# Expert stage in quads of experts with column groups of 32, and a ring of 1 MB halves

## The chip, the cores and the metric

The kernel runs on one core of one Trainium2 chip. The metric is the device time of one execution, in microseconds.

## What is computed

The reference is one inference step of a two-layer decoder trunk for 256 prompt tokens and 8 decode tokens, model width 1024, all in f32. Layer 0 mixes tokens with GLA and Mamba-2, layer 1 with HGRN2. After each mixer comes a mixture of experts: 16 experts in four routing groups of four, each token goes to two experts of its best group. Only this part is touched by the change:

```python
for e in range(N_EXPERTS):                       # 16
    he = jax.nn.silu(t @ w_gate[e]) * (t @ w_up[e])   # 1024 -> 512
    y = y + gates[:, e:e + 1] * (he @ w_down[e])      # 512 -> 1024
x = layer_norm(ALPHA * x + y, ...)
```

The weights of one expert are three matrices of 2 MB (2.10 million bytes), those of a layer 96 MB in 48 matrices, or 96 halves of 1 MB (1,048,576 bytes).

## The kernel before

Each engine runs its own program and they meet at semaphores. SyncE (SP) issues all weight loads in program order (`fill`, L337; `fill_half`, L346): a load first waits until its place is free, and whatever stands behind it on SP waits too. The places are the six 2 MB slots of `ring` (`PLACE`) and, in the expert stages alone, a seventh, `EXTRA`, in the buffer `A`.

An expert stage (`experts`, PE) runs like this. After layer norm the router's scores are turned into places: five small matmuls count, for each token, its row among the tokens of its expert (`moe_places`), `keep_clock(4)` issues eight filler instructions (L1180), DVE builds one-hot matrices `SLOT1` (L2303). `gather` (L1205, four per layer, each for four experts) multiplies them with the tokens; the result is `xg`, 64 rows for each expert: 56 for prompt tokens, 8 for the decode tokens. The 16 experts are worked in eight pairs; the two experts of a pair lie in the two column groups of 64 of the array. A pair is `gate_up` (L1220, 64 instructions: a f32 matmul is two instructions), `turn_hidden` (L1229, four transposes), `down` (L1244, 32 instructions), with the `scatter` of the previous pair (L1259, 16 instructions) in two halves around `turn_hidden`. `scatter` multiplies the pair's 128 result rows with `PT`, the transposed gate weights, over all 264 tokens, in eight chunks; DVE adds each chunk to `xacc` (L2410, eight instructions of 264 columns a pair). In every second pair the `gather` for the next four experts stands ahead of `down`. `turn_weights` builds `PT` in the first pair.

After the last pair DVE takes the row means of the result (`centred_copy`), DVE and ACT copy it without its mean to `Y`, the last `scatter` runs, ACT squares `xacc` chunk by chunk and PE sums the squares (L1143), and the layer norm follows. Weights of the next stage (`w_c`) are issued by SP behind those of the experts; all but the first of them wait for the layer norm (`norm_roots`).

## Time and profile before

| | us |
|---|---|
| median of 3 runs (lowest to highest) | 989.76 (989.46 to 990.78) |
| span of the profiled execution | 988.7 |
| PE busy in it | 952.2 (96%) |
| DVE / ACT / POOL busy | 400.9 / 281.5 / 103.6 |
| DMA moved | 299.64 MB, mean 303 GB/s |
| chain that ended last: PE / DMA / DVE | 78% / 10% / 7% |

The span is the time from the first to the last instruction; the median of the runs is 1.1 us longer. Matmuls overlap one another, so that the busy time of a group of instructions is less than count times mean. Of a group's cost on PE the chain's pieces tell more: they are laid end to end. The first expert stage lies at about 304 to 544 us of the span, the second at 741 to 981 us.

### The profile page before, as it was taken

What the parts mean: (1) busy time and instruction counts of PE and PEld (TensorE: products, weight loads), DVE (VectorE), ACT (ScalarE), POOL (GpSimd) and SP (SyncE); (2) the same over time, 40 slices, a digit from 0 to 9 for tenths busy, and PEclk for the clock granted to TensorE, in tenths of its full rate; (3) what the DMA queues carried; (4) which work ended last, traced back from release to release, by engine and by line L of the source; (5) the groups of instructions that cost most, each with busy time, mean ns of one, the idle gap of its engine ahead of it and who ended that gap; (6) DMA issues with size and microseconds to landing.
All of it is one profiled execution on the core that took longest, in us unless ns stands there. A gap on an engine that the chain in (4) does not pass through costs nothing.

```text
span 988.7 us, 12651 instructions
## 1 busy us (share of the span) xinstructions
PE 952.2 (96%) x4923; PEld 609.8 (62%) x4923; DVE 400.9 (41%) x973; ACT 281.5 (28%) x603; POOL 103.6 (10%) x167
## 2 busy tenths in 40 slices
PE   8999999899999999999998999999999999999995
PEld 6777777677876354545435877777875444545433
DVE  2468886954127021212116336675244111212134
ACT  3534434223024110101002258886133010101003
POOL 2222223361000000000000000113100000000000
PEclk9999999999999999999999999999999999999998
DMA  9943545966843999999993954342885999999981
GB/s 380 357 193 134 191 161 171 407 266 266 340 164 147 423 410 422 421 423 420 421 422 153 409 221 174 152 149 71 329 352 237 421 413 421 420 422 420 422 351 45
DMA packets 38991, 299.64 MB, mean 303 GB/s; under 512 B 4808, under 2 KB 6344, under 8 KB 8456
## 3 DMA queue, kind: packets, MB, share of 16 engines
q1 hardware_dynamic: 33696, 268.52, 66.7%
q0 software_dynamic: 4544, 29.65, 7.8%
q8 instruction: 43, 0.70, 0.3%
q10 hardware_dynamic: 688, 0.60, 0.2%
q14 instruction: 20, 0.16, 0.0%
HBM read 283.32 MB, written 15.53 MB: 302 GB/s over the span
## 4 chain that ended last, share of the span: by engine, by line
PE 78%; DMA 10%; DVE 7%; ACT 3%; issue 2%; POOL 0%; ACTq 0%; DVEq 0%; POOLq 0%
PE bank L1220 20%; PE bank L1244 10%; PE bank L1390 7%; PE bank L856 7%; PE bank L1103 6%; PE bank L1259 6%; PE bank L1205 5%; PE bank L1377 4%; DMA ring<-in_w_up 4%; PE bank L1124 3%; PE bank L1143 2%; DVE ring L2093 1%; DMA W<-in_conv_cols 1%; DMA spread<-xd_rows 1%; DMA spread<-v_rows 1%
## 5 line engine op out<-in xcount | busy, mean ns | idle before, releaser
L1220 PE MATMUL bank<-ring,A 128*64 128x512 f32 x880 | 223.0, 592 | 1.0 <-DMA ring<-in_w_up 1.0
L856 PE MATMUL bank<-xT,ring 128*128 128x264 f32 x704 | 165.0, 390 | 1.7 <-DMA ring<-in_w_ab 1.3
L856 PEld LDWEIGHTS bank<-xT,ring 128*128 128x128 f32 x704 | 132.0, 191 | 32.3 <-issue 8.9
L1220 PEld LDWEIGHTS bank<-ring,A 128*64 128x64 f32 x880 | 72.5, 137 | 123.8 <-issue 123.1
L1244 PE MATMUL bank<-ring,W 128*64 128x512 f32 x448 | 113.8, 596 | 0.9 <-ACT W L1741 0.9
L2364 DVE TENSOR_TENSOR W<-W,bank 128x512 f32<-128x512 f32 x16 | 11.0, 688 | 200.3 <-PE bank L1220 200.3
L1390 PE MATMUL bank<-xT,ring 128*128 128x264 f32 x320 | 78.0, 391 | 0.0
L1244 PEld LDWEIGHTS bank<-ring,W 128*64 128x64 f32 x448 | 34.8, 137 | 60.4 <-issue 59.3
L1259 PE MATMUL bank<-W,A 128*128 128x264 f32 x256 | 66.9, 408 | 3.9 <-ACT A L1733 3.9
L1390 PEld LDWEIGHTS bank<-xT,ring 128*128 128x128 f32 x320 | 58.3, 190 | 11.1 <-issue 1.6
L1220 PE MATMUL bank<-A 128*64 128x512 f32 x144 | 63.4, 592 | 0.7 <-DMA ring<-in_w_up 0.7
L1259 PEld LDWEIGHTS bank<-W,A 128*128 128x128 f32 x256 | 48.5, 199 | 24.5 <-issue 11.4
L2410 DVE TENSOR_TENSOR W<-W,bank 128x264 f32<-128x264 f32 x128 | 54.3, 428 | 12.5 <-PE bank L1259 11.3
L1103 PE MATMUL bank<-A,ring 128*128 128x264 f32 x256 | 57.4, 386 | 0.3 <-ACT A L1472 0.3
L781 POOL TENSOR_SCALAR xT<-xT,vecs 128x264 f32<-128x264 f32 x4 | 5.6, 1398 | 492.7 <-DVE xT L2214 492.7
L1103 PEld LDWEIGHTS bank<-A,ring 128*128 128x128 f32 x256 | 48.6, 190 | 8.8 <-ACT A L1472 0.6
L1720 ACT ACTIVATE W<-bank 128x512 f32<-128x512 f32 x16 | 9.6, 597 | 145.2 <-PE bank L1220 145.2
L1205 PE MATMUL bank<-A,W 128*128 128x224 f32 x256 | 49.9, 353 | 0.6 <-DVEq L2312 0.6
L2374 DVE COPY A<-bank 128x512 f32<-128x512 f32 x14 | 9.7, 692 | 99.0 <-PE bank L1244 99.0
L1205 PEld LDWEIGHTS bank<-A,W 128*128 128x128 f32 x256 | 48.3, 190 | 1.4 <-DVEq L2312 1.0
L1377 PE MATMUL bank<-xT,ring 128*128 128x264 f32 x192 | 44.6, 396 | 2.6 <-ACT xT L1663 2.6
L1724 ACT COPY W<-bank 128x512 f32<-128x512 f32 x16 | 9.4, 585 | 124.0 <-PE bank L1229 124.0
(339 smaller groups left out, 1147.2 us busy)
## 6 DMA issues: line engine op xcount, KB each, us to landing
ring<-in_w_gate SPq DMA_DIRECT2D x56, 1024.0 KB, 13.8
ring<-in_w_down SPq DMA_DIRECT2D x56, 1024.0 KB, 14.0
ring<-in_w_up SPq DMA_DIRECT2D x54, 1024.0 KB, 16.8
ring<-in_w_ab SPq DMA_DIRECT2D x10, 2048.0 KB, 8.4
ring<-in_w_c SPq DMA_DIRECT2D x8, 2048.0 KB, 11.2
A<-in_w_up SPq DMA_DIRECT2D x10, 1024.0 KB, 14.3
ring<-in_w_oab SPq DMA_DIRECT2D x4, 2048.0 KB, 10.4
A<-in_w_gate SPq DMA_DIRECT2D x8, 1024.0 KB, 13.2
```

The source lines that it names most:

```text
L856: mm = pe.matmul(ab_bank(m)[:, 0:T], slot(AB_IN0 + m // 4, 8)[:, c, (m % 4) * P:(m % 4 + 1) * P], xT[:, c, :], start=(c == 0), stop=(c == ...
L1103: mm = pe.matmul(out_bank(m)[:, 0:T], w[:, c, (m % 2) * P:(m % 2 + 1) * P], src, start=(c == 0), stop=(c == 15))
L1124: mm = pe.matmul(out_bank(m)[:, 0:T], w[:, c, (m % 4) * P:(m % 4 + 1) * P], A[:, 16 + c, :], start=(c == 0), stop=(c == 7))
L1143: mm = pe.matmul(square_bank(k)[:, 0:T], ones[:, :], lnsq[:, c, :], start=(c == 0), stop=(c == DC - 1))
L1205: mm = pe.matmul(gather_bank(i)[:, c * 4 * PCAP:(c + 1) * 4 * PCAP], xtm[:, b, (2 * i + c) * P:(2 * i + c + 1) * P], SLOT1[:, b, 4 * g:4 * ...
L1220: mm = pe.matmul(bank[i][64 * j:64 * j + 64, :], xg[:, 2 * (pair % 2) + j, c, :], slot(n0 + 6 * pair + 2 * i + j, 8)[:, c, :], start=(c == ...
L1244: mm = pe.matmul(bank[4 + i][64 * j:64 * j + 64, :], hT[:, f * P + CAP * j:f * P + CAP * (j + 1)], slot(n0 + 6 * pair + 4 + j, 8)[:, 4 * i ...
L1259: pe.matmul(back_bank(c)[:, 0:T], Y[:, c * P:(c + 1) * P], PT[:, pair, :], start=True, stop=True).then_inc(sem("moe_back"), 1)
L1377: mm = pe.matmul(c_bank(m)[:, 0:T], slot(n, 8)[:, c, i * P:(i + 1) * P], xT[:, c, :], start=(c == 0), stop=(c == DC - 1))
L1390: mm = pe.matmul(c_bank(m)[:, 0:T], slot(c_in(m // 4), 8)[:, c, (m % 4) * P:(m % 4 + 1) * P], xT[:, c, :], start=(c == 0), stop=(c == DC - 1))
L2364: dve.tensor_tensor(hid, hid, bank[1][:, :], ALU.mult).then_inc(sem("moe_hidden"), 1)
L2410: dve.tensor_tensor(xacc[:, c, :], xacc[:, c, :], back_bank(c)[:, 0:T], ALU.add).then_inc(sem("moe_added"), 1)
```

## The change

The 16 experts are worked in four quads. A quad holds one expert of each routing group, and each has one of four column groups of 32. The prompt tokens are taken in two blocks of 128, and each block goes through the array by itself: an expert has 32 rows for a block, 28 for prompt tokens and 4 for half of the decode tokens (before: 56 and 8 for all). If an expert gets more prompt tokens of a block than 28, an overflow path runs, as it did before above 56; no expert gets more than 25 of a block with these inputs. The places come from two matmuls in place of five. A gather has 112 columns moving in place of 224, a scatter matmul 136 in place of 264 (one block and the decode tokens); there are as many of each. Up to three scatter chunks share a bank, and DVE adds them with two instructions, one for the block's tokens and one for the decode tokens.

On PE a quad is now `gate_up(q, 0)`, `gate_up(q, 1)`, `turn_hidden` of block 0, `gather(q + 1)`, `turn_hidden` of block 1, `down` in two halves, `scatter(q)`. The mean that the layer norm needs ahead of the last scatter moves in front of the last quad's up projection.

The weight ring has 1 MB halves as its unit. Twenty places ("homes") take the first twenty halves of a layer: twelve in `ring`, five in `A`, one each in `spread`, in the place of `xacc` and in that of `Y`; the last two are used once, so the ring then goes round over 18. Half k waits for the read of the group of four halves in which half k-18 lies. The first loads wait for the ends of the users of those buffers in the mixer (`home_free`).

```diff
-CAP = 64
-PCAP = CAP - NB
-PLIM = PCAP
-DR = 64
+QUADS = E_N // E_G
+ROWS = P // E_G
+DCAP = NB // 2
+PCAP = ROWS - DCAP
+SPREAD_N = P + NB
+SCATTER = ((0, 3), (3, 6), (6, 8))
...
-        EXTRA = Aflat[:, 7232:7232 + SLOT_W]
...
+        MOE_HALVES = 6 * E_N
+        QUAD_HALVES = MOE_HALVES // QUADS
+        A_HOMES, SPREAD_HOME, XACC_HOME, Y_HOME = range(12, 17), 17, 18, 19
+        FIRST_HOMES = [
+            [XACC_HOME, Y_HOME, SPREAD_HOME, 12, 14, 15, 8, 9, 10, 11, 4, 5, 6, 7, 2, 3, 0, 1, 13, 16],
+            [XACC_HOME, Y_HOME, 4, 5, 6, 7, SPREAD_HOME, 12, 13, 15, 16, 2, 3, 0, 1, 8, 9, 10, 11, 14]]
+        FIRST_ORDER = [list(range(20)), [2, 3, 4, 5, 0, 1] + list(range(6, 20))]
+        CYCLE = len(FIRST_HOMES[0]) - 2
+        HOMES = [[h[k] if k < 2 else h[2 + (k - 2) % CYCLE] for k in range(MOE_HALVES)] for h in FIRST_HOMES]
+        FILLS = 6
...
+        def halves_read(layer, q, i, half):
+
+            return 6 * (QUADS * layer + q) + 2 * i + half + 1
...
+        def down_bank(i, b):
+
+            return bank[4 + b] if i else up_bank(b)
+
+        def back_bank(n):
+
+            return bank[2 + n % 2]
...
+            def home_free(layer, home):
+
+                if home < 2 * SLOTS:
+                    slot_free = ({4: ("states_stored", 64), 5: ("states_stored", 64), 2: ("out0_ready", 2), 3: ("out0_ready", 4),
+                                  1: ("out0_ready", 6), 0: ("out0_ready", 8)},
+                                 {2: ("in1_ready", 28), 3: ("in1_ready", 32), 1: ("states_stored", 96), 0: ("states_stored", 96),
+                                  4: ("out1_ready", 4), 5: ("out1_ready", 8)})
+                    return [slot_free[layer][home // 2]]
+                if layer == 0:
+                    if home in (13, 16):
+                        return [("out0_ready", 8)]
+                    return [("ssd_outputs_read", 4), ("heads_gated", 4), ("ssd_p_stored", 32)]
+                if home == 14:
+                    return [("out1_ready", 8)]
+                return [("heads_gated", 12), ("heads_prompt_state_stored0", 16 * 6), ("heads_prompt_state_stored1", 16 * 6)]
+
+            def fill_expert(layer, k):
+
+                q, r = divmod(k, QUAD_HALVES)
+                i, r = divmod(r, 8)
+                half, g = divmod(r, 4)
+                home = HOMES[layer][k]
+                if k < len(FIRST_HOMES[layer]):
+                    for name, value in home_free(layer, home):
+                        sp.wait_ge(sem(name), value)
+                else:
+                    sp.wait_ge(sem("moe_read"), MOE_HALVES // 4 * layer + (k - CYCLE) // 4 + 1)
+                src = expert_views(layer, bass.ds(E_G * g + q, 1))[i]
+                n = halves_read(layer, q, i, half) - 1
+                sp.dma_start(home_of(home), src[:, HALF_W * half:HALF_W * (half + 1)]).then_inc(
+                    sem(f"moe_filled{n % FILLS}"), 16)
...
+        xg = area(2112, DC, 2 * E_G, ROWS)
+        xacc = area(4160, DC, T)
+        Y = area(6272, 2, D)
+        PT = area(8320, 2 * QUADS, SPREAD_N)
...
-                pe.matmul(bank[3][:, 0:16], strict[:, :], chosen[:, 0, :], start=True, stop=True)
-                for i, last in enumerate((strict[:, :], ones[:, :])):
-                    pe.matmul(bank[3][:, 16 + 16 * i:32 + 16 * i], ones[:, :], chosen[:, 0, :], start=True, stop=False)
-                    mm = pe.matmul(bank[3][:, 16 + 16 * i:32 + 16 * i], last, chosen[:, 1, :], start=False, stop=True)
-                mm.then_inc(sem("moe_places"), 1)
+                pe.matmul(bank[3][:, 0:2 * E_N], strict[:, :], chosen[:, 0:2, :], start=True, stop=True)
+                pe.matmul(bank[3][:, 2 * E_N:4 * E_N], ones[:, :], chosen[:, 0:2, :], start=True, stop=True).then_inc(
+                    sem("moe_places"), 1)
                 keep_clock(4)
-                def gather(g):
+                L0 = QUADS * layer
...
                         for c in range(2):
                             for b in range(2):
-                                mm = pe.matmul(gather_bank(i)[:, c * 4 * PCAP:(c + 1) * 4 * PCAP],
+                                at = (2 * c + b) * E_G * PCAP
+                                mm = pe.matmul(gather_bank(i)[:, at:at + E_G * PCAP],
                                                xtm[:, b, (2 * i + c) * P:(2 * i + c + 1) * P],
-                                               SLOT1[:, b, 4 * g:4 * g + 4, 0:PCAP], start=(b == 0), stop=(b == 1))
+                                               SEL[:, q, b, :, 0:PCAP], start=True, stop=True)
                         mm.then_inc(sem("gather_ready"), 1)
...
+                def gate_up(q, i):
+
+                    for half in range(2):
+                        expert_ready(pe, layer, q, i, half)
+                        w = [expert_half(layer, q, i, half, g) for g in range(E_G)]
+                        for b in range(2):
+                            out = up_bank(b) if i else gate_bank(b)
+                            for c in range(4 * half, 4 * half + 4):
+                                if i == 0 and b == 0 and c % 2 == 0:
+                                    pe.wait_ge(sem(f"xg_copied{c // 2 % 2}"), 2 * (L0 + q) + c // 4 + 1)
+                                for g in range(E_G):
+                                    mm = pe.matmul(out[ROWS * g:ROWS * (g + 1), :], xg[:, c, E_G * b + g, :], w[g][:, c % 4, :],
+                                                   start=(c == 0), stop=(c == DC - 1))
+                            if b == 0 and half == 1:
+                                mm.then_inc(sem("block_done"), 1)
+                        mm.then_inc(sem("moe_read"), 1)
...
+                def down(q, i):
+
+                    expert_ready(pe, layer, q, 2, i)
+                    w = [expert_half(layer, q, 2, i, g) for g in range(E_G)]
+                    for b in range(2):
+                        if i == 0:
+                            pe.wait_ge(sem("hT_copied"), 2 * (L0 + q) + b + 1)
+                        elif q + 1 < QUADS:
+                            pe.wait_ge(sem(f"xg_copied{b}"), 2 * (L0 + q + 1) + 1)
                         for f in range(4):
-                            for j in range(2):
-                                mm = pe.matmul(bank[4 + i][64 * j:64 * j + 64, :], hT[:, f * P + CAP * j:f * P + CAP * (j + 1)],
-                                               slot(n0 + 6 * pair + 4 + j, 8)[:, 4 * i + f, :],
+                            for g in range(E_G):
+                                mm = pe.matmul(down_bank(i, b)[ROWS * g:ROWS * (g + 1), :],
+                                               hT[:, b, f * P + ROWS * g:f * P + ROWS * (g + 1)], w[g][:, f, :],
                                                start=(f == 0), stop=(f == 3))
-                        mm.then_inc(sem("moe_down"), 1)
-                        if pair == PAIRS - 1 and i == 0:
-                            pe.wait_ge(sem("norm_ahead"), 3 * layer + 2)
-                            pe.matmul(mean_bank(2 * layer + 1)[:, 0:T], mean_ones[:, :], late_sums[:, 0, :],
-                                      start=True, stop=True).then_inc(sem("norm_sum"), 1)
-
...
+                        mm.then_inc(sem("moe_read" if b else "block_done"), 1)
...
+                def scatter(q):
+
+                    for b in range(2):
+                        for j, (c0, c1) in enumerate(SCATTER):
+                            n = 6 * q + 3 * b + j
+                            if j < 2:
+                                y_ready(q, b, j)
+                            if b == 0 and j < 2 and q + 1 < QUADS:
+                                pe.wait_ge(sem(f"xg_copied{j}"), 2 * (L0 + q + 2))
+                            if n >= 2:
+                                pe.wait_ge(sem("moe_added"), 48 * layer + 2 * (n - 1))
+                            for c in range(c0, c1):
+                                mm = pe.matmul(back_bank(n)[:, (c - c0) * SPREAD_N:(c - c0 + 1) * SPREAD_N],
+                                               Y[:, b, c * P:(c + 1) * P], PT[:, 2 * q + b, :], start=True, stop=True)
+                            mm.then_inc(sem("moe_back"), 1)
...
+                for q in range(QUADS):
+                    gate_up(q, 0)
+                    if q == 0:
+                        turn_weights()
+                        flag = pe.value_load(over[0:1, 0:1], min_val=0, max_val=1)
+                    if q + 1 == QUADS:
+                        pe.wait_ge(sem("norm_ahead"), 4 * layer + 2)
+                        pe.matmul(mean_bank(2 * layer + 1)[:, 0:T], mean_ones[:, :], late_sums[:, 0, :],
+                                  start=True, stop=True).then_inc(sem("norm_sum"), 1)
+                    gate_up(q, 1)
+                    turn_hidden(q, 0)
+                    if q + 1 < QUADS:
+                        gather(q + 1)
+                    turn_hidden(q, 1)
+                    down(q, 0)
+                    down(q, 1)
+                    scatter(q)
...
+                def centred_copies():
+
+                    q = QUADS - 1
+                    for i in range(2):
+                        dve.wait_ge(sem("block_done"), 4 * (L0 + q) + i + 3)
+                        st.add(dve.tensor_reduce(row_means[:, 0, i:i + 1], down_bank(i, 0)[:, :], AX, ALU.add))
+                        if i:
+                            block_mean(0)
+                        dve.wait_ge(sem("moe_read"), halves_read(layer, q, 2, i))
+                        st.add(dve.tensor_reduce(row_means[:, 1, i:i + 1], down_bank(i, 1)[:, :], AX, ALU.add))
+                    block_mean(1)
+                    dve.tensor_scalar(Y[:, 1, 0:512], down_bank(0, 1)[:, :], row_means[:, 1, 2:3], None, ALU.add).then_inc(
+                        sem("y_copied1"), 1)
...
+                def add_back(q):
+                    for b in range(2):
+                        for j, (c0, c1) in enumerate(SCATTER):
+                            n = 6 * (L0 + q) + 3 * b + j
+                            dve.wait_ge(sem("moe_back"), n + 1)
+                            if n >= 3:
+                                dve.wait_ge(sem("moe_added"), 2 * (n - 2))
+                            back = back_bank(n)[:, 0:(c1 - c0) * SPREAD_N].rearrange("p (c t) -> p c t", t=SPREAD_N)
+                            for part, of in ((slice(P * b, P * (b + 1)), slice(0, P)), (slice(NP, T), slice(P, SPREAD_N))):
+                                dve.tensor_tensor(xacc[:, c0:c1, part], xacc[:, c0:c1, part], back[:, :, of], ALU.add).then_inc(
+                                    sem("moe_added"), 1)
```

## Rows read from the trace of the kernel before

**Rows 1.** The profile page, part 2: the span in 40 equal slices of 24.7 us, in tenths.
```profile
DMA  9943545966843999999993954342885999999981
```

**Rows 2.** The chain that ended last, by pieces in order of time: start us, us, what.
```profile
423.36 13.73 PE bank L1220 x64
...
462.04 1.98 PE bank L1259 x8
...
466.24 6.05 PE bank L1205 x32
472.29 7.02 PE bank L1244 x32
479.31 13.76 PE bank L1220 x64
...
747.22 13.88 PE bank L1220 x64
```

**Rows 3.** Timeline of PE around both expert stages: start us, us, line; idle before in brackets.
```profile
297.96 2.40 PE L1180 MATMUL bank<-causal,ident 128*128 128x128 f32 x20
304.03 6.32 PE L1205 MATMUL bank<-A,W 128*128 128x224 f32 x32 [0.31 <-DVEq L2312]
310.28 13.95 PE L1220 MATMUL bank<-ring,A 128*64 128x512 f32 x64
515.56 3.65 PE L1220 MATMUL bank<-ring,A 128*64 128x512 f32 x16 [1.00 <-DMA ring<-in_w_up]
527.57 3.65 PE L1244 MATMUL bank<-ring,W 128*64 128x512 f32 x16
533.18 5.51 PE L1259 MATMUL bank<-W,A 128*128 128x264 f32 x16 [1.96 <-ACT A L1733]
538.53 3.72 PE L1143 MATMUL bank<-A,ones 128*128 128x264 f32 x16
964.16 3.65 PE L1244 MATMUL bank<-ring,W 128*64 128x512 f32 x16
976.32 3.83 PE L1143 MATMUL bank<-A,ones 128*128 128x264 f32 x16 [1.03 <-ACT A L1674]
```

**Rows 4.** Windows around the experts: length, busy time and count of each engine, PEclk, DMA share, GB/s.
```profile
300.00:310.00 10.00, 8.60 (x53) 8.22 (x52) 8.72 (x28) 3.87 (x9) 1.44 (x1) 1.00 0.01 4
450.00:500.00 50.00, 50.00 (x240) 24.36 (x237) 10.57 (x23) 4.88 (x9) 0.00 (x0) 1.00 1.01 421
700.00:750.00 50.00, 47.56 (x261) 39.14 (x261) 25.73 (x72) 15.88 (x28) 3.84 (x8) 1.00 0.77 313
```

**Rows 5.** Timeline of SP's DMA issues ahead of the two expert stages.
```profile
247.10 2.06 SPq L346 DMA_DIRECT2D ring<-in_w_gate  x4
...
289.07 0.70 SPq L346 DMA_DIRECT2D A<-in_w_gate  x1
313.98 0.33 SPq L346 DMA_DIRECT2D ring<-in_w_gate  x1
700.59 0.33 SPq L346 DMA_DIRECT2D A<-in_w_up  x1
```

**Rows 6.** The source view of L346, its last line, for a load of 1 MB.
```profile
DMA to landing us min/median/max: 5.0/14.6/25.7
```

**Rows 7.** PE around line 1079, four column groups of 32 with 512 columns moving.
```profile
186.23 1.92 PE L1079 MATMUL bank<-ring,W 128*32 128x512 f32 x16 [1.81 <-DVE ring L2093]
188.09 2.05 PE L856 MATMUL bank<-xT,ring 128*128 128x264 f32 x8
```

**Rows 8.** One-us windows of PE after the first expert stage: length, busy, PEclk, DMA share, GB/s.
```profile
534.00:535.00 1.00, 1.00 (x4) 0.58 0.00 0
537.00:538.00 1.00, 1.00 (x5) 0.71 0.00 0
```

**Rows 9.** Groups of instructions kept apart by shape: busy us, mean ns, idle before.
```profile
L2387 DVE TENSOR_TENSOR W<-W,bank 128x2112 f32<-128x2112 f32 x2 | 4.7, 2354 | 0.0
L2410 DVE TENSOR_TENSOR W<-W,bank 128x264 f32<-128x264 f32 x128 | 54.3, 428 | 12.5 <-PE bank L1259 11.3
```

More of the change, by code:

```diff
@@ L358, in fill_over, with fill_experts @@
+            def fill_experts(layer):
+                for k in FIRST_ORDER[layer]:
+                    fill_expert(layer, k)
+                for k in range(len(FIRST_ORDER[layer]), MOE_HALVES):
+                    fill_expert(layer, k)
             def fill_over(layer):
@@ L377, in _ @@
                 sp.dma_start(xT[:, c:c + 4, :], x_cols[:, c:c + 4, :]).then_inc(sem(f"x_loaded{c // 4}"), 16)
-            for half in range(2):
-                fill_half(AB_IN0, half, w_ab[0])
+            fill_first(w_ab[0])
             for g in range(11):
@@ new lines, in turn_weights @@
+                def turn_weights():
+                    pe.wait_ge(sem("moe_weighted"), layer + 1)
+                    for r in range(2 * QUADS):
+                        out = bank[(4, 5, 2)[r // 3]][:, (r % 3) * SPREAD_N:(r % 3 + 1) * SPREAD_N]
+                        pe.transpose(out[:, 0:P], WS[:, r * P:(r + 1) * P], ident[:, :])
+                        tr = pe.transpose(out[:, P:SPREAD_N], WS2[:, r * P:(r + 1) * P], ident[0:NB, 0:NB])
+                    tr.then_inc(sem("pt_turned"), 1)
@@ L2382, in sum_ahead @@
                     dve.sem_inc(sem("norm_ahead"), 1)
+                    dve.wait_ge(sem("norm_sum"), 4 * layer + 3)
+                    st.run(minus_mean())
                 def minus_mean():
@@ new lines, in experts @@
+                flag = dve.value_load(over[0:1, 0:1], min_val=0, max_val=1)
+                for q in range(QUADS):
+                    hidden(q)
+                    if q + 1 < QUADS:
+                        for i in (1, 3):
+                            gathered(dve, affine, i, L0 + q + 1)
+                        copies(q)
+                    else:
+                        centred_copies()
+                    add_back(q)
+                    if q + 2 == QUADS:
+                        sum_ahead()
@@ L2422, in experts @@
+                dve.wait_ge(sem("moe_added"), 12 * (L0 + QUADS))
                 with dve.If(flag > 0):
```

467 lines of the change are left out of this document (195 added, 272 removed).

## Prediction

> **What bounds the kernel now.** I read four views in this order. The slices of the page first [rows 1]: the DMA engines are full (9) in two long stretches, slices 13 to 20 and 31 to 37, which are the two expert stages, and mostly idle in the slices just ahead of each. The windows say the same in numbers: 0.01 of the DMA engines at 300 to 310 us and 0.77 at 700 to 750, and 421 GB/s at full share inside [rows 4]. Then the chain, for what PE does meanwhile [rows 2]: inside the stage it is PE, pieces laid end to end. Two pairs last 479.31 - 423.36 = 55.95 us: twice 13.73 (gate and up), 7.02 (down) and 4.20 (scatter and turning, 466.24 - 462.04), and once 6.05 (gather). Last the timeline, for what PE waits for [rows 3]: in all of the stage it stood still on a load just once, for 1.00 us, on the last up matrix.
>
> So the two run level. At 421 GB/s a half of 1,048,576 bytes takes 2.49 us (2.5 below), a pair's twelve halves 29.9 us, while PE needs 28.0 us on average. PE gains some 2 us on the loads with each pair, and the seven slots (14 halves) loaded ahead are used up just in the last pair. From the first gate matmul (310.28) to the end of the last down (527.57 + 3.65 = 531.22) it is 220.9 us. Whoever makes only PE faster meets the loads. What can shorten the stage is more weights loaded in the idle DMA time ahead of it; a faster PE is needed beside it.
>
> **The change: what PE does in a quad.** Gate and up are 256 instructions in fours. The nearest row is the same shape, four groups of 32 with 512 columns: 16 instructions from 186.23 to the next at 188.09, less the first load (0.1, an estimate) 0.43 to 0.46 us a four [rows 7]; I take 0.43, by which the old pair's 32 twos also go (13.73 / 32); at 0.46 PE would end the stage, at 211, 3 us a layer later. So 64 x 0.43 = 27.5 us, the same as two pairs now. Down is 32 fours, taken at twice the old 7.02 = 14.0 us. Turning is eight transposes, 0.12 each as below, 0.9. A gather has half the columns, but a full 128 x 128 load for each instruction; with 128 columns moving, twenty take 2.40 us, 0.12 each [rows 3], so 32 x 0.12 = 3.8 us in place of 6.05. The ends are 3.0 (by columns alone) and 6.05 (the old row, [rows 2]); the twenty are nearest in shape. Scatter is 32 instructions, again 3.8 us, in place of two pairs' 2 x 4.20 less the turning, 7.5. DVE's share of it: its cost goes as 0.155 us + 1.04 ns a column (428 ns for 264, 2354 for 2112 [rows 9]). Three chunks of 128 are 0.55 us and of 8 are 0.18, two chunks 0.42 and 0.17, so two blocks cost 2 x (2 x 0.73 + 0.59) = 4.1 us, in two alternating banks behind its last copy: I take 4.5 us for the scatter. Sum: 27.5 + 14.0 + 0.9 + 3.8 + 4.5 = 50.7 us in place of 55.95. Turning the gate weights is 16 transposes, 2 us, in quad 0.
>
> **The start.** Three count matmuls fewer are six instructions of 0.12, 0.7 us, and one one-hot instruction fewer on DVE hides behind the filler matmuls. The first gather is 2.5 us shorter. The first gate matmul thus comes some 3.4 us earlier, at 306.8 in place of 310.28. ACT and DVE copy the gathered tokens two chunks at a time beside it, and the first weights have long landed.
>
> **The loads, layer 0.** Before, 14 halves are in place, the last of them issued at 289.07 and the next only at 313.98, when the first read ends [rows 5]. Now twenty. The new first waits (`ssd_p_stored` and its like) hold SP, with all twenty halves and the overflow check queued behind, until the mixer's last stores. Before, SP began at 247.10 [rows 5], when its states were stored; sixteen halves (40 us) fit between that and 289, when the last out-projection read opens the last four homes. Their loads take 10 us, so all twenty are in by about 300, before 306.8. Six halves more, 15 us of DMA, lie in idle time.
>
> From here I count from the first gate matmul. Groups of four halves are read at 7.0 and 13.9 us. Halves 20 and 21 may start at 7.0, the next only at 13.9; a lone half lands 5.0 us after its issue, of which 2.5 is transfer [rows 6]. So group 5 (halves 20 to 23) is complete at 13.9 + 2.5 + 5.0 = 21.4, and each further group 10.0 us later: group 23, the last down halves, at 201.4. PE by itself would start that group at 3 x 50.7 + 2 + 27.5 + 0.9 + 0.7 + 7.0 = 190.3. (The 0.7 is the wait for block 1's hidden rows, which in the last quad no gather covers.) So loads end the stage: PE waits about 3 us before several groups of the last quad, and the last down ends at 201.4 + 7.0 = 208.4, or 515.2 us of the span. PE has 11 us in hand, so its prices may be wrong by 5% without moving the end.
>
> **Those waits and the clock.** After 1.96 us of idle PE at 531 to 533 the granted clock is at half, 1.2 of 2.4 GHz, from about 534.2 to 537.6 [rows 8], and sixteen instructions take 5.51 us [rows 3] in place of the 3.7 of a scatter (4.20 less four transposes, [rows 2]); after the wait of 1.00 us nothing is lost, 3.65 us for sixteen [rows 3]. So waits of 3 us will halve the clock for a while. In the middle this costs nothing, as PE then waits less for the next group; before the last group it costs about 1.75 us (3.4 us at half). I take half: 0.9. The stage ends at 516.1 in place of 531.2: 15.1 us saved.
>
> **Layer 1.** Before, four halves are out by 700.59 [rows 5]; the other sixteen need 40 us of DMA, and other transfers 12 more (313 GB/s for 50 us [rows 4] is 15.7 MB, of which ten halves are 10.5; 5.2 MB at 421 are 12 us). From 700 the DMA engines are thus busy until 752. The first gate matmul moves from 747.2 [rows 2] to 743.8, so group 1 is read at 757.7, halves 20 and 21 land by 757, and group 5 is complete at 765.2, the last at 945.2, the last down 0.9 late at 953.1. Before it was 964.16 + 3.65 = 967.8 [rows 3]. 14.7 us saved. This uses the times of before for what lies ahead and adds to layer 0's gain, which carries through: the mixer between is a chain of PE, and the first `w_c` load waits for nothing new.
>
> **The tail.** Before, from the end of the last down to the end of the squares' sum it is 542.25 - 531.22 = 11.0 us, and 980.15 - 967.8 = 12.3 in layer 1 [rows 3]: a wait of 1.96, a scatter of 5.5 and 3.7 of sums among it. Now block 0's rows are ready while down runs on block 1, and scatter starts without a wait. DVE comes free some 2.0 us after down (two reductions' work and a copy), adds six pieces in 4.1 us, PE's last chunks end at about 5.8, the sums (32 instructions of 0.12) at 9.6. Saved 1.5 and, with the second copy's wait gone, 2 us; if the clock falls here too, nothing.
>
> **Sum.** 15.1 + 14.7 + 1.5 + 2.0 = 33.3 us of the span of 988.7, so 955.4, and with the 1.1 us by which the runs' median lies above the span, 956.5 us.
>
> The rivals.
> - **A refill that stumbles.** SP's waits, at most two groups ahead, may leave the DMA engines short gaps that the old, finer order did not. Half of the six halves' gain lost would be 2 x 7.5: 971. Against it: 4 groups lie between a home's read and its next use, 40 us of loads. 0.15.
> - **No more ahead than before.** If the first homes open late (layer 0's wait for stores) SP holds all twenty behind them. Then 15 us a layer go: 986. The order suits the dates known, so 0.07.
> - **PE sets the end after all.** If the loads run ahead (a gap less at the start, up to 427 GB/s), the end is PE's, 8 to 11 us a layer earlier at most: 938. No row shows more than 421 over 50 us. 0.06.
> - **Clock at half through the last quad (slower).** Every group then lasts 14.0 us against 10.0 of loads. From group 20, which comes at 171.4: 185.4, 199.4, 215.9, 229.9 us; 21 us a layer more than 208.4, so 998. It decides from 17 us a layer. Against it: the clock came back within 4 us of steady work [rows 8]. 0.05. The Trainium skill, "TensorE: Matmul & The Clock Gate", section HAM oscillation, tells of a kernel in which each short burst of matmuls after a DMA wait started with a gated clock, every time. By that rule this rival would be the likeliest; the trace's own bursts here are 7 us, not 2, and agree with it only for the start of a burst.
> - **Fours that do not overlap (slower).** If over a long run each four shows one weight load, 0.12 us more as in the twenty, 0.55 a four, then a quad is 96 x 0.55 + 9.2 = 62 us, longer than its loads, the last down ends at 2 + 4 x 62 - 4.5 = 245.5, and that is 37 us a layer above 208.4: 1030. It decides from 0.50 us a four. The row has only sixteen in sequence. 0.05. The Trainium skill, "TensorEngine Tiling (Array Packing)", section PSUM Bottleneck, warns that evacuation may become the bound after such packing; here DVE has 4.1 us of adds, four instructions of 512 columns (0.69) and four of 224 (0.39) in a quad of 50 us, and ACT as many without the adds, so I give it no price.
>
> **How the numbers follow.** The forecast has 0.60, its own range 948 to 965 (both clock losses, 0.46 a four, the start). The rivals above have 0.15, 0.07, 0.06, 0.05 and 0.05, 0.02 is left for no change. A measurement here can tell 0.2% (2 us) from no change: faster 0.88, same 0.02, slower 0.10. The range of 8 in 10 takes the forecast, the stumbling refill and most of the PE case: 942 to 973.
>
> **What would show it.** Right: PE idle, with DMA as its releaser, about 1 to 3 us before four or five groups in the last quad of each layer; DMA at 421 GB/s without a gap from 21 us after the first gate matmul to the end of the loads; a quad of about 51 us on PE until then; the last loads about 15 us earlier. Wrong: more than 0.45 us a four, DMA gaps inside the stage, fewer than twenty halves in at the first gate matmul, or PE never waiting for DMA.

## The result and the profile after

The changed kernel takes 966.22 us (median of 4 runs, 963.58 to 969.02), beside 989.61 us for the kernel before on the same chip: ratio 0.976, interval 0.974 to 0.979, so 23.4 us less. The forecast was 956.5 us, in a range of 942 to 973. The profiled execution took 964.11 us, with a span of 962.3. One execution of the kernel before, beside the first four experiments, took 1662.55 us at a granted clock of 0.556, and no median or ratio below counts it.

The slices of the profile page of the changed kernel, for [rows 1]; a slice is 24.1 us here:

```profile
DMA  9953453985983999999993954343799999999951
```

The two long stretches of full DMA engines are still there. Ahead of them the idle time is used: slice 12 has gone from 4 to 8 (layer 0's loads ahead), slice 31 from 5 to 9 (layer 1's).

The chain that ended last, of the changed kernel, for [rows 2] (start us, us, what). Its lines are: L1266 gather, L1282 gate and up, L1306 down, L1332 scatter, L1205 the sums of squares.

```profile
301.43 3.83 PE bank L1266 x32
305.25 13.87 PE bank L1282 x128
...
359.57 27.61 PE bank L1282 x256
...
391.76 13.87 PE bank L1306 x128
410.44 27.65 PE bank L1282 x256
440.69 28.37 DMA ring<-in_w_gate
469.10 7.12 PE bank L1282 x64
481.84 26.93 DMA A<-in_w_down
508.82 7.12 PE bank L1306 x64
...
727.10 13.87 PE bank L1282 x128
...
900.48 29.98 DMA ring<-in_w_down
930.50 8.81 PE bank L1306 x64
947.84 5.44 PE bank L1205 x32
```

A quad lasts 410.44 - 359.57 = 50.87 us on PE, where a pair of pairs lasted 55.95. In the last quad the chain goes over to DMA, at 440.69 and 481.84 and again at 900.48. The last group of loads is there 508.82 - 305.25 = 203.6 us after the first gate matmul, in layer 1 930.50 - 727.10 = 203.4.

The waits of PE in the changed kernel, summed up (total us, times, longest):

```profile
PE bank L1282 <- DMA ring<-in_w_up: 8.5, 4, 2.9
PE bank L1306 <- DMA A<-in_w_down: 4.2, 2, 2.8
...
PE bank L1205 <- issue: 3.0, 1, 3.0
PE bank L1306 <- DMA ring<-in_w_down: 2.8, 1, 2.8
...
PE bank L1282 <- DMA ring<-in_w_gate: 0.8, 1, 0.8
...
PE bank L1282 <- DMA A<-in_w_gate: 0.5, 1, 0.5
```

Where [rows 3] had one wait of 1.00 us for a load, there are now nine in the five groups of DMA, 16.8 us, all in the last quads: five in layer 0 and four in layer 1. The timeline of PE at the two ends, for the end of [rows 3] (start us, us, line; idle before in brackets):

```profile
515.82 1.66 PE L1332 MATMUL bank<-W 128*128 128x136 f32 x12
518.40 3.04 PE L1332 MATMUL bank<-W 128*128 128x136 f32 x20 [0.92 <-DVE W L2498]
521.28 3.80 PE L1205 MATMUL bank<-W,ones 128*128 128x128 f32 x32
...
947.84 5.42 PE L1205 MATMUL bank<-W,ones 128*128 128x128 f32 x32 [3.02 <-issue]
```

And the windows, for [rows 4] and [rows 8] (length, PE busy and its count, PEclk, DMA share, GB/s):

```profile
296.00:298.00 2.00, 2.00 (x20) 1.00 0.80 336
300.00:310.00 10.00, 9.77 (x90) 1.00 0.01 2
...
312.00:314.00 2.00, 2.00 (x24) 1.00 0.39 66
318.00:320.00 2.00, 2.00 (x17) 1.00 0.54 221
330.00:332.00 2.00, 2.00 (x24) 1.00 0.96 320
450.00:500.00 50.00, 44.06 (x374) 0.97 1.01 421
700.00:750.00 50.00, 47.65 (x365) 1.00 0.99 410
480.00:481.00 1.00, 1.00 (x12) 0.50 1.02 426
948.00:950.00 2.00, 2.00 (x10) 0.50 0.04 8
```

The loads made ahead end at 298 us; up to 312 DMA stands still; then the refill starts, with dips at 318 and at 330 us. In layer 1 the share from 700 to 750 us is 0.99 in place of 0.77. So the stage is bound by its loads, as forecast, and it is shorter, since more was loaded in idle time: from the first gate matmul to the end of the last down it was 220.9 and 220.6 us, and is 515.94 - 305.25 = 210.7 and 939.31 - 727.10 = 212.2.

### The profile page after: what moved, and what is told of

It is laid out like the page before. It is cut to its first block, busy times and chain, and to the rows that moved or that the text cites. A ratio compares the mean times of both kernels' runs of the same rounds, so it can differ in the third digit from the quotient of the medians.

```text
span 962.3 us, 15639 instructions
## 1 busy us (share of the span) xinstructions
PE 910.4 (95%) x6463; PEld 561.9 (58%) x6463; DVE 372.9 (39%) x947; ACT 278.4 (29%) x591; POOL 103.7 (11%) x168
## 4 chain that ended last, share of the span: by engine, by line
PE 68%; DMA 17%; DVE 8%; ACT 2%; issue 2%; SPq 1%; POOL 1%; ACTq 0%; DVEq 0%; POOLq 0%
PE bank L1282 19%; PE bank L1459 8%; PE bank L1306 7%; PE bank L911 7%; PE bank L1158 6%; PE bank L1446 5%; DMA A<-in_w_gate 3%; DMA ring<-in_w_down 3%; DMA ring<-in_w_gate 3%; DMA A<-in_w_down 3%; PE bank L1179 3%; PE bank L1332 3%; PE bank L1266 2%; DVE ring L2173 1%; DMA spread<-v_rows 1%
## 5 line engine op out<-in xcount | busy, mean ns | idle before, releaser
L1282 PE MATMUL bank<-ring,W 128*32 128x512 f32 x1312 | 184.8, 603 | 6.8 <-DMA ring<-in_w_up 6.3
L911 PEld LDWEIGHTS bank<-xT,ring 128*128 128x128 f32 x704 | 131.3, 190 | 31.4 <-issue 8.5
L1282 PE MATMUL bank<-A,W 128*32 128x512 f32 x544 | 119.3, 593 | 3.0 <-DMA ring<-in_w_up 2.2
L1282 PEld LDWEIGHTS bank<-ring,W 128*32 128x32 f32 x1312 | 51.1, 111 | 103.5 <-issue 93.0
L1306 PE MATMUL bank<-ring,A 128*32 128x512 f32 x672 | 99.6, 604 | 4.2 <-DMA ring<-in_w_down 2.8
L1306 PE MATMUL bank<-A 128*32 128x512 f32 x304 | 70.2, 593 | 0.0
L1459 PEld LDWEIGHTS bank<-xT,ring 128*128 128x128 f32 x320 | 58.3, 190 | 11.1 <-issue 1.6
L1306 PEld LDWEIGHTS bank<-ring,A 128*32 128x32 f32 x672 | 27.1, 111 | 56.0 <-issue 50.5
L1282 PE MATMUL bank<-spread,W 128*32 128x512 f32 x128 | 56.3, 593 | 0.0
L1282 PEld LDWEIGHTS bank<-A,W 128*32 128x32 f32 x544 | 31.2, 110 | 35.6 <-issue 31.1
L1446 PEld LDWEIGHTS bank<-xT,ring 128*128 128x128 f32 x192 | 37.1, 195 | 9.8 <-issue 2.6
L1332 PE MATMUL bank<-W 128*128 128x136 f32 x256 | 37.9, 292 | 2.7 <-DVE W L2498 1.8
L1332 PEld LDWEIGHTS bank<-W 128*128 128x128 f32 x256 | 31.9, 189 | 13.8 <-issue 8.1
```

Of the source, the lines that this page charges most:

```text
L911: mm = pe.matmul(ab_bank(m)[:, 0:T], slot(AB_IN0 + m // 4, 8)[:, c, (m % 4) * P:(m % 4 + 1) * P], xT[:, c, :], start=(c == 0), stop=(c == ...
L1282: mm = pe.matmul(out[ROWS * g:ROWS * (g + 1), :], xg[:, c, E_G * b + g, :], w[g][:, c % 4, :], start=(c == 0), stop=(c == DC - 1))
L1306: mm = pe.matmul(down_bank(i, b)[ROWS * g:ROWS * (g + 1), :], hT[:, b, f * P + ROWS * g:f * P + ROWS * (g + 1)], w[g][:, f, :], start=(f = ...
L1332: mm = pe.matmul(back_bank(n)[:, (c - c0) * SPREAD_N:(c - c0 + 1) * SPREAD_N], Y[:, b, c * P:(c + 1) * P], PT[:, 2 * q + b, :], start=True ...
L1446: mm = pe.matmul(c_bank(m)[:, 0:T], slot(n, 8)[:, c, i * P:(i + 1) * P], xT[:, c, :], start=(c == 0), stop=(c == DC - 1))
L1459: mm = pe.matmul(c_bank(m)[:, 0:T], slot(c_in(m // 4), 8)[:, c, (m % 4) * P:(m % 4 + 1) * P], xT[:, c, :], start=(c == 0), stop=(c == DC - 1))
```

## The experiments

All are edits of the changed kernel, and each computes the same result; where unused matmuls are added, they go to a bank that nobody reads then, and this is said. A stage is counted from the first gate matmul to the end of the last down (L0 and L1 for the two layers). The first four ran beside the kernel before at 989.14 us, the next four beside 990.05, the last three beside 988.65.

**Fourteen homes in place of twenty.** Only the loads made ahead are taken back; the quads stay.

```diff
-            [XACC_HOME, Y_HOME, SPREAD_HOME, 12, 14, 15, 8, 9, 10, 11, 4, 5, 6, 7, 2, 3, 0, 1, 13, 16],
+            [XACC_HOME, Y_HOME, 8, 9, 10, 11, 4, 5, 6, 7, 2, 3, 0, 1],
...
-        FIRST_ORDER = [list(range(20)), [2, 3, 4, 5, 0, 1] + list(range(6, 20))]
+        FIRST_ORDER = [list(range(14)), [2, 3, 4, 5, 0, 1] + list(range(6, 14))]
```

> The changed kernel with only 14 homes (the ring's twelve halves, xacc and Y), as many halves loaded ahead as before; quads and PE work untouched. Theory (loads end the stage; what the change gained is the six more halves loaded in idle time): the last down halves land 6 x 2.5 = 15 us later in each layer, so about 15 us later end of each expert stage, 30 us in all, near 994 us, a little above the kernel before; PE waits for DMA 20 us or more a layer. Rival (the lighter gather and scatter on PE gave the gain): within 3 us of the changed kernel's 966.

Measured: 995.4 us (median of 8, 993.51 to 999.58), ratio 1.007 (1.004 to 1.009) to the kernel before. Its chain:

```profile
307.42 13.87 PE bank L1282 x128
...
415.47 21.01 DMA ring<-in_w_up
...
444.98 22.77 DMA ring<-in_w_down
...
476.24 21.30 DMA ring<-in_w_up
497.59 7.12 PE bank L1282 x64
506.04 21.27 DMA ring<-in_w_down
527.36 8.81 PE bank L1306 x64
```

From 415 us on nearly every group ends in a DMA, and PE waits 22.2 and 19.1 us for loads. The stage is 228.75 us in L0 and 225.5 in L1, 18.1 and 13.3 longer than with twenty. So without the six halves nothing of the gain is left: the faster quads alone, with their coarser ring, give none.

With fourteen halves loaded ahead, as before, the quads are even 7.8 and 4.9 us slower than the pairs (220.9 and 220.6). The last load lands 219.9 and 218.3 us after the first gate matmul, before 215.1 and 214.7. These 4.8 and 3.6 us are lost for the most part at the first refills, where DMA has dips at 320 to 324 and at 332 us; from then on a group lands about every 9.9 us, a few excepted. Homes come free four halves at a time and not two, and two of the fourteen are used only once (before, all fourteen went round); these two causes aren't told apart. The rest stands behind the last load: 8.8 and 7.2 us of down work, where before it was 5.8 and 5.9; of the 8.8, 1.7 us is the clock.

**PE slowed, with twenty homes and with fourteen.** After the scatter of quads 0 to 2 unused matmuls are put in: 10, or 22 (4.91 us, by which a quad is as long as the old pairs).

```diff
                     scatter(q)
+                    if q + 1 < QUADS:
+                        keep_clock(22)
```

> The changed kernel with 20 filler instructions (0.12 us each, 2.4 us) on PE behind the scatters of quads 0 to 2, 7.2 us more PE work in each layer. Theory (PE has about 6.6 us in hand per layer: 8.3 us of DMA waits less 1.75 of clock): no more than 1 us a layer later, and the waits for DMA in the last quad nearly gone; 964 to 968 us. Rival (PE bounds): 14 us more, 980.

> The changed kernel with 44 filler instructions (5.3 us) behind the scatters of quads 0 to 2, which gives PE the pace that it had before, 56 us for four experts; twenty homes. Theory: 15.8 us more PE work a layer, of which 6.6 are covered: 9 us later in each layer less up to 1.75 of clock, about 980 to 984 us; no waits for DMA on PE. Rival (the lighter PE work gave everything): 988 or more. Rival (prefetch gave everything): 966.

> Both: 14 homes and the fillers of 5.3 us. Theory: with 14 homes PE has 6.6 + 15 = 21.6 us in hand, more than the 15.8 of fillers, so no later than with 14 homes alone, about 991 to 995 us. If the two parts simply added it would be 966 + 30 + 18 = 1010.

Measured: 972.02 us (967.81 to 974.01) with ten, 972.0 (968.74 to 972.75) with 22, and 999.19 (997.49 to 1002.85) with 22 and fourteen homes. With ten, the last group of L0 starts 510.43 - 306.35 = 204.1 us after the first gate matmul, 0.5 later than in the changed kernel, and the stages are 211.2 and 212.3 us: the work is hidden, as expected. The whole was expected at 964 to 968 and missed this, and 8.3 of the 16.8 us of waits for loads are left, where they should have nearly gone. The longer time lies outside the stages: 214.6 us between them in place of 211.2 (a wait of 1.81 us, below, and layer 1's first gather at half clock, 5.45 us in place of 3.83), a start 1.1 us later and a tail 1.5 us longer. With 22 the chain is PE's to the end:

```profile
306.83 13.87 PE bank L1282 x128
...
492.14 13.92 PE bank L1282 x128
507.54 13.92 PE bank L1306 x128
```

The stage is 214.6 us in both layers, 3.9 and 2.4 more for 14.7 us of work put in. I had expected 9: I had taken the clock's loss off the room that PE has, where it must be added, since a PE that never waits never loses it. The room is 14.7 - 3.9 = 10.8 us in L0 and 12.3 in L1. With fourteen homes the same 14.7 us cost 1.9 and 2.0 (stages of 230.6 and 227.5): the effects don't add, and DMA is the bound. I had expected no cost at all there and at most 995 us. In L0 a new dip of DMA stands at 372 to 376 us, and the last down takes 10.00 us in place of 8.81; what of the 1.9 us each makes wasn't tried.

The fillers stand behind three of the four quads, so this is not quite the old pace: the last quad keeps the new one. With 4.9 us more in it the stage would be 219.5 us, an estimate from these rows, and nearly all of its gain gone. Twenty homes with the old pairs were not run.

**The dips at the start of the refill.** The changed kernel's last group lands 2 us later than forecast, and DMA has the dips at 318 to 322 and at 330 us above. Two edits were tried alone, then together. One puts the homes that are used only once (`xacc`, `y`) at halves 4 and 5, so that all four halves of group 0 open homes. The other moves the turning of the gate weights from behind the first expert's up halves to between them, so that the first up half is read without the turning, 3.3 us, ahead of it. (The first also lets ACT write `xacc` a group later; the second reads the overflow flag in quad 1.)

```diff
-        HOMES = [[h[k] if k < 2 else h[2 + (k - 2) % CYCLE] for k in range(MOE_HALVES)] for h in FIRST_HOMES]
+        HOMES = [[home_at(h, k) for k in range(MOE_HALVES)] for h in FIRST_HOMES]
...
                     for half in range(2):
                         expert_ready(pe, layer, q, i, half)
+                        if (q, i, half) == (0, 1, 1):
+                            turn_weights()
...
-                    if q == 0:
-                        turn_weights()
```

> The changed kernel with the two homes that are used once (xacc and Y) taken by halves 4 and 5 in place of 0 and 1, so that the first group read (7 us after the first gate matmul) sets free four homes in place of two; ACT writes xacc one group later. Theory (the end follows from when the loads may start again): the DMA engines lose no 2 us gap at 13 us after the first gate matmul, and the last down ends about 2 us earlier in each layer (208.5 to 209 us after the first gate matmul in place of 210.7 in layer 0). Rival (the gap is made good later, since SP has four groups in hand): no change of the stage's length.

> The changed kernel with the turning of the gate weights (3.3 us of PE) moved from ahead of the first quad's up projection to between its two halves, so that up half 0 is read 3.3 us earlier. PE's work is the same. Theory: halves 26 and later may start 3.3 us earlier, a gap of about 1.5 us in the loads around 24 us after the first gate matmul goes, the stage ends 1 to 1.5 us earlier in each layer. Rival (only PE's total work counts): no change.

> Both edits of the two kernels before it that gained nothing alone: the four halves used once stand in the second group, so the fifth quarter-megabyte pair of homes comes free after the first four reads, and the turn of the routing weights is put between the two up halves of the first expert. Theory (the 2 us that the last group lands late come from the dips of the queue at 312 to 330 us, and each edit alone only moved the dip from the one wait to the other): no dip below 405 GB/s between 318 and 335 us, last group 200 to 202 us after the first gate matmul in place of 203.6, stage 2 to 3 us shorter per layer, whole 960 to 963 us. Rival (the rate after the dip, 410 GB/s, is what sets the landing, or the queue makes the dip good): last group again at 203 to 204 us, whole 964 to 967.

> The changed kernel once more, beside the two others of this call on one chip, so that they are compared with it and not with a run of another chip. Expected: 964 to 968 us; last group of each layer 203.6 us after the first gate matmul; tail of layer 1 (end of the last down to end of the square sums) 13 to 14 us.

Measured, with the time at which the last group starts after the first gate matmul in L0 and L1:

| | median us (range) | last group |
|---|---|---|
| changed kernel, first chip | 966.22 (963.58 to 969.02) | 203.6, 203.4 |
| homes alone | 964.96 (963.51 to 968.92) | 203.7, 203.5 |
| turning alone | 965.62 (964.16 to 969.3) | 203.8, 203.1 |
| changed kernel again | 967.83 (964.58 to 968.63) | 205.3, 204.3 |
| both | 962.83 (960.41 to 964.5) | 202.0, 202.1 |

The chain of the kernel with both edits (its first gate matmul is at 304.95):

```profile
479.81 27.10 DMA A<-in_w_down
506.96 7.12 PE bank L1316 x64
```

Each alone leaves one of the two dips and gains nothing: with the homes alone it lies at 330 us, with the turning alone at 320. The landings of single loads in the trace say the same. Group 5 (halves 20 to 23) and group 6 are complete 21.5 and 33.2 us after the first gate matmul of layer 0 in the changed kernel, 20.9 and 32.9 with the homes alone, 21.9 and 32.7 with the turning alone, and 21.0 and 30.9 with both. Both together leave no dip, and the last group lands some 1.4 us sooner. The whole is 5.0 us faster than the changed kernel on the same chip; only 2 x 1.4 of it is this. The rest differs from run to run: the start of the first stage (304.95 in place of 307.23) and the clock.

**No jump ahead of the last sums.** In layer 0 the sums of squares stand in the branch that PE takes (`flag < 1`); in layer 1 behind the overflow code, over which PE jumps. The edit puts layer 1's in the branch too.

```diff
...
-                if layer == 0:
-                    with pe.If(flag < 1):
-                        norm_squares(1)
+                with pe.If(flag < 1):
+                    norm_squares(2 * layer + 1)
+                    if layer == 0:
                         settle_over()
                 over_experts(layer, flag)
-                if layer == 1:
-                    norm_squares(3)
```

> The changed kernel with the sums of the squares of layer 1 issued in the branch that is taken when nothing overflows, as in layer 0, so that PE doesn't jump over the overflow code between the last scatter and the sums. Theory (PE's idle time of 3.0 us there, which the profile puts to issue, is fetching instructions behind the jump): this idle time goes to about 1 us, the clock isn't lowered behind it, 2 to 4 us less from the last down to the end of the sums in layer 1 (14.0 us in the changed kernel, 9.2 in layer 0). Rival (PE waits there for the squares or for the clock): unchanged.

Measured: 961.66 us (961.08 to 962.25), ratio 0.972 (0.969 to 0.975). Its timeline of PE at the end of layer 1:

```profile
946.41 3.80 PE L1205 MATMUL bank<-W,ones 128*128 128x128 f32 x32
```

The wait of 3.02 us is gone, and so is the slow clock behind it (3.80 us in place of 5.42). From the end of the last down to the end of the sums it is 950.21 - 941.06 = 9.2 us, in the changed kernel 953.26 - 939.31 = 14.0. In the changed kernel one packet of the instruction queue falls into that wait; this is the queue's row of DMA at 944 to 948 us:

```profile
q8 instruction: 1, 0.02, 1.4%
```

Without the jump there is none from 936 to 948 us. The wait is that for the code on the other side of the jump.

**The clock kept through the last quad.** Unused matmuls, 8, 10, 4 and 10 calls of two instructions, ahead of the two up and the two down halves of quad 3, where PE waits for loads.

```diff
...
+                        if (q, i, half) == (3, 1, 1):
+                            keep_clock(10, 3)
...
+                        keep_clock(8, 3)
...
+                    if q + 1 == QUADS:
+                        keep_clock(4, 3)
                     down(q, 0)
+                    if q + 1 == QUADS:
+                        keep_clock(10, 3)
                     down(q, 1)
```

> The changed kernel with filler matmuls (16, 20, 8 and 20 instructions of 0.12 us) in the last quad ahead of up half 0, up half 1, down half 0 and down half 1, where PE waits for loads. Theory (waits above 2 us lower the clock, and before the last group that costs 1.7 us): the granted clock stays full through the last quad in both layers, and layer 1's last down takes 7.1 in place of 8.8 us; 1.7 us less in layer 1, none in layer 0, where its last down was at full clock. Rival (the clock falls whatever PE does between the waits): unchanged.

Measured: 973.28 us (969.99 to 973.43). The stages are 210.9 and 210.8 us, and the last down takes 7.12 us in both layers, against 8.81 in layer 1 of the changed kernel: as expected, and layer 1's stage is 1.4 us shorter. Yet the whole is 7 us slower than 966.22, and 5.5 slower than the changed kernel on the same chip (967.83). Between the stages it takes 218.8 us in place of 211.2. This is PE at the start of the second mixer:

```profile
536.40 11.95 PE L1453 MATMUL bank<-xT,ring 128*128 128x264 f32 x42 [3.68 <-issue]
```

It is the jump again, this time over layer 0's overflow code: one instruction packet comes at 527 to 528 us, the next only at 534 to 535, when DMA is at 415 GB/s with the `w_c` loads. If the instructions that the first brings are few, PE runs dry. The kernel with ten fillers has the same gap (1.81 us at 532.9), the changed kernel and the one with 22 fillers have none. How many instructions are left behind the jump depends on how many stand ahead of it; that is my reading, from these four and the next kernel, and is not shown.

**Everything together.** Homes, turning, no jump, and only 16 unused matmuls in the last quad of a layer, a number chosen so that many instructions of a packet are left behind the jump.

```diff
+                        if (q, i, half) == (3, 1, 1):
+                            keep_clock(6, 3)
...
+                    if q + 1 == QUADS:
+                        keep_clock(10, 3)
                     down(q, 1)
```

> The start of the last kernel, the sums of layer 1 in the branch that is taken (no jump ahead of them), and 16 unused matmuls in the last quad of each layer ahead of the second up half and the last down half, which fill waits of PE for the loads. Theory: tail of layer 1 9.2 us in place of 14.0; the last down of both layers 7.1 us for 64 (full clock) where the changed kernel has 8.8 in layer 1; no gap of PE over 1.5 us for want of instructions at the start of the mixer of layer 1, since only 64 instructions lie between the jump and it; with the start's gain 954 to 958 us, without it 958 to 961. Rival (the fillers cost more than the clock gives back, or the code's place brings a fetch gap again): 962 to 968 us.

Measured: 957.03 us (953.11 to 958.65), ratio 0.967 (0.965 to 0.970) to the kernel before; on the same chip the changed kernel took 967.83. It is the fastest of all.

```profile
482.62 28.48 DMA A<-in_w_down
511.14 7.12 PE bank L1318 x64
...
900.18 29.89 DMA ring<-in_w_down
930.11 7.12 PE bank L1318 x64
942.74 3.65 PE bank L1213 x32
```

Both last downs run at full clock, the last sums follow 9.2 us behind in layer 1, and PE has no wait for instructions at the start of the second mixer.

**What differs from run to run.** The changed kernel's two profiled executions have spans of 962.3 and 966.9 us. The second started its first gate matmul 2.0 us later, and has a slow piece in the chain and a slower last down:

```profile
307.23 13.87 PE bank L1282 x128
324.41 15.57 PE bank L1282 x128
...
512.57 8.77 PE bank L1306 x64
```

Its windows there (length, PE busy and its count, PEclk, DMA share, GB/s):

```profile
322.00:324.00 2.00, 2.00 (x11) 1.00 0.97 238
324.00:326.00 2.00, 2.00 (x14) 0.70 0.98 414
326.00:328.00 2.00, 2.00 (x12) 0.50 1.04 438
328.00:330.00 2.00, 2.00 (x24) 0.95 0.98 414
```

The clock goes to half though PE had not been idle. What PE did just before was the turning of the gate weights: sixteen transposes, every second one on an 8 x 8 block, in 3.3 us up to 324.4. The fall begins at 324.8. This costs 1.70 us, and as these are the first reads, which open homes, the last group starts 205.3 us after the first gate matmul and not 203.6. The kernel with everything has the same at 331 to 335 us, again 0.4 us behind the end of the turning (8.70 us for 64 in place of 7.00), and its last group starts at 204.5 in L0 against 201.9 in L1. In no other trace does a fall follow the turning, so why it does in these two stays open. With the later start and the last down's 1.65 the three make 5.3 us at the end of the stage of L0 (521.34 in place of 515.94), all of the difference between the two spans and a little more.

## Why the prediction was right, and where it was off

The measured 966.2 us lie in the range of 8 in 10, but 1.2 us above the forecast's own range, 948 to 965. The mechanism came as told; what was off are sizes.

- **What bounds the stage: right.** Fourteen homes give back 18.1 and 13.3 us of the stage, fillers of 14.7 us a layer cost 3.9 and 2.4. The forecast had the last down of layer 0 end at 516.1, and it ended at 515.94, 15.3 us earlier than before; of these 10.2 lie inside the stage and 5.0 ahead of it. The first gate matmul came at 305.25, forecast 306.8: 1.85 us of the 5.0 were there at 226 us already, most of it by the clock, and are no work of the change. That is luck: without it the end would have been 1.7 us late. The other 3.2 are the sum of the two terms given for the start, 0.7 and 2.5; the 3.4 that was taken is more than its terms.
- **A quad on PE: right.** Forecast 27.5 + 14.0 + 0.9 + 3.8 + 4.5 = 50.7, measured 50.87: 27.6 for gate and up (0.43 a four), 13.87 for down, 3.56 for a gather and 4.8 for the scatter. "PE has 11 us in hand" was 10.8 and 12.3, and this hides two misses of one size: by the kernel with 22 fillers PE alone would start the last group at 192.9 us (an estimate, its 207.6 less 14.7), not at 190.3 (the turning took 3.3 us where 2 was set), and the loads came 2.2 later as well. The sum for 0.46 a four, 211, and that for fours that do not overlap, 245.5, hold a gather in the last quad, which has none; they should be some 3 us less.
- **The loads made ahead: right.** In layer 0 the twentieth half lands at 299.5 us, forecast 300.
- **The last group: 2 us too early.** Forecast 201.4 us after the first gate matmul, measured 203.6 and 203.4. The first term held: group 5 was complete at 21.5 and 21.6, forecast 21.4, so the dip at 318 us was in the sum. The step that failed is "each further group 10.0 us later". Group 6 came 11.7 and 11.3 us behind group 5: this is the dip at 330 us. Two of its halves wait until the third group is read, and that was at 24.2 us, behind the turning; with the 2 us that the turning was priced at it would have been 22.9, an estimate. The two were issued at once and landed 6.5 and 8.6 us later. Then a group landed every 9.8 to 10.1 us, but for one of 10.9 (10.8 in layer 1) and one of 10.4 (10.3). With both edits at the start group 6 comes 9.9 us behind group 5, and the last group starts at 202.0 and 202.1. So the rival of the refill that stumbles came in small: 1.7 and 1.3 us a layer, not 7.5. Why single groups late in the stage take 10.3 to 10.9 us stays open.
- **The clock: the size right on average, the place open.** Forecast 0.9 for the last down, half of 1.75. Measured 0.0 and 1.7 in one execution, 1.65 and 0.0 in the other, and 2.9 once with the turning moved alone (10.02 us for 64). The rival with the clock at half through the last quad did not come: after waits of 2.2 to 2.9 us it is at half for some 3.4 us, at 480 us for instance, and not always (7.12 us for 64 behind the wait of 2.8 at 508.82). The Trainium skill, "TensorE: Matmul & The Clock Gate", section HAM oscillation, tells of bursts of some 2 us behind DMA waits of 3 to 5 us, and there every one starts slow. Here three of the five bursts behind waits of 2.2 to 2.9 us lose clock, and a burst of 7 us comes back to full speed within itself.
- **The tail of layer 0: right.** Forecast 9.6 us from the last down to the end of the sums, measured 9.1.
- **The tail of layer 1: the largest miss.** Forecast 10.3, measured 14.0. I had taken over its wait of 1.03 us [rows 3] as ACT's, and layer 0's shape for the rest. The term that was missing is the code behind a jump: 3.0 us of wait for instructions, and then 1.6 us in the slow clock. Without the jump it is 9.2. Before, two such packets fell into 973 to 978 us, beside a wait of 1.03 us: its fetch was the same, but it lay beside the slow scatter and the wait for ACT. That last is argued, and was not tried on the kernel before.
- **The sum.** Forecast span 955.4, measured 962.3: 6.9 us, of which the end of layer 1's last down is 939.31 - 936.5 = 2.8, its tail 3.7, and the rest 0.4. (With the 1.85 us of luck taken out, the 2.8 are 4.7, of which 1.7 lie at the end of layer 0's stage and 2.9 in layer 1's.) The median lies 3.9 us above this span, where I had 1.1. An execution takes 1.8 us more than its own span (964.11 and 962.3), and the other 2.1 are that the profiled one is quick among runs that spread over 5.4 us; the clock's dips are enough to make such a spread (above). From one profiled execution this can't be foreseen; the range has to hold it.

## What to carry to other kernels

Where two engines run level through a stage, work out the stage from both sides: here the faster engine bought nothing without the loads made in the idle time ahead, and by the estimate above most of their gain needs the faster engine beside them. Count when a buffer comes free, in the unit in which it comes free, and what the reader does just before it frees it: the coarser ring lost 5 to 8 us a layer with as many halves loaded ahead, and 3.3 us of turning ahead of a read cost 1.7 of loads. And before you add instructions or end a stage with code behind a branch, look in the profile for waits with no releaser and for packets of the instruction queue in them: they cost 3 us here, 5 with the clock, and went away by moving three lines.

## What the runs showed of the hardware

- A jump over code that is not taken can cost a fetch of instructions through the DMA engines: 3.0 us of idle PE with idle DMA engines (944 to 948 us), and 3.68 in layer 0 of the kernel with fillers in the last quad. The second packet comes 3.0 us behind the first in layer 1, where the DMA engines are idle, and 6.2 in layer 0, where the `w_c` loads run; that the loads hold it up is my reading. The Trainium skill, "DMA: Bandwidth & Descriptors", section Issuing engines are not separate DMA queues, says that DMAs started by the scalar, sync or gpsimd engine run on the same 16 DMA engines and interleave. It does not name the instruction packets, which in this trace stand among the DMA queues as q8.
- The granted clock fell to half for 3.4 us amid work without a pause (from 324.8 and from 331.1 us), both times 0.4 us behind the turning of the gate weights, beside the falls after a wait. It cost 1.7 us each time. After 22 other passes of the same turning it did not fall.
- Four column groups of 32 with 512 columns each take 0.43 us a four over 128 and 256 instructions in sequence (13.87 and 27.6 us), no more than two groups of 64 took for a two.
